# Folding two tiles of squares on VectorE before one ones product, and rounded dummy products in three waits

## The reference, cut to what matters

```python
def rmsnorm(x, g):
    x32 = x.astype(jnp.float32)
    y = x32 * lax.rsqrt(jnp.mean(x32 * x32, axis=-1, keepdims=True) + EPS)
    return (y * g.astype(jnp.float32)).astype(x.dtype)
...
    o = rmsnorm(o_f + o_b, out_g).reshape(B, S, GLA_V)   # 4 heads of 256 values each
    o = o * jax.nn.silu(r.astype(f32))
    return o.astype(h.dtype) @ w_o
```

## Time and profile before

| | |
|---|---|
| runs | 1992.94, 1994.84, 1995.06 us, median 1994.84 |
| profiled execution, span from first to last instruction | 1992.7 us |
| its own time beside the span | none is given apart from the runs; the fastest run is 0.2 us above the span |
| TensorE busy | 1970.7 us, 99% |
| VectorE, ScalarE, GpSimd busy | 57%, 38%, 30% |
| mean granted TensorE clock | 0.998 of full |

### The profile page before, as it was taken

How to read it: one execution, slowest core, us unless ns; L and a number is a source line. 1 busy time by engine, 2 the same in 40 slices (tenths; PEclk the granted TensorE clock), 3 DMA queues, 4 the chain that set the end, 5 groups by cost and what they waited for, 6 DMA issues and landing times.

```text
span 1992.7 us, 24353 instructions
## 1 busy us (share of the span) xinstructions
PE 1970.7 (99%) x9570; PEld 1626.7 (82%) x9570; DVE 1137.4 (57%) x1153; ACT 759.4 (38%) x867; POOL 588.6 (30%) x520
## 2 busy tenths in 40 slices
PE   9999999999999999999999999999999999999998
PEld 7766788888887988888888878788888888888886
DVE  6797355555556547454555466872335474545456
ACT  6665332222234534332322234355553353232223
POOL 1100279997000000289995012522310000000000
PEclk9999999999999999999999999999999999999999
DMA  7300144443223230154443232412123312223231
GB/s 232 101 22 1 63 149 169 153 162 104 102 85 115 86 105 24 66 188 161 143 160 110 96 105 91 117 49 79 64 85 106 106 45 104 102 87 105 84 106 64
DMA packets 32832, 204.01 MB, mean 102 GB/s; under 512 B 3952, under 2 KB 4080, under 8 KB 10096
## 3 DMA queue, kind: packets, MB, share of 16 engines
q1 hardware_dynamic: 25712, 168.83, 24.6%
q0 software_dynamic: 7040, 34.08, 5.4%
HBM read 191.89 MB, written 2.10 MB: 97 GB/s over the span
## 4 chain that ended last, share of the span: by engine, by line
PE 93%; DVE 3%; ACT 2%; issue 1%; DMA 0%; POOL 0%; SPq 0%; POOLq 0%; DVEq 0%; ACTq 0%
PE ps L261 24%; PE ps L263 24%; PE ps L262 24%; PE ps L697 2%; PE ps L2473 2%; PE ps L2474 2%; PE ps L2475 2%; PE ps L1713 1%; PE ps L684 1%; PE ps L293 1%; PE ps L292 1%; PE ps L291 1%; PE ps L1697 1%; PE ps L673 1%; PE ps L672 1%
## 5 line engine op out<-in xcount | busy, mean ns | idle before, releaser
L223 ACT ACTIVATE w_hi<-w_raw 128x2048 fp32r<-128x2048 f32 x142 | 272.4, 1918 | 714.7 <-PE ps L263 643.3
L231 DVE TENSOR_TENSOR w_lo<-w_raw,w_hi 128x2048 fp32r<-128x2048 f32 x139 | 323.2, 2325 | 118.3 <-ACT w_hi L223 116.2
L261 PE MATMUL ps<-h_hi,w_hi 128*128 128x512 f32 (+1 forms) x976 | 383.2, 393 | 4.1 <-DVE w_lo L231 3.0
L263 PE MATMUL ps<-h_hi,w_lo 128*128 128x512 f32 (+1 forms) x976 | 373.5, 383 | 0.0
L262 PE MATMUL ps<-h_lo,w_hi 128*128 128x512 f32 (+1 forms) x976 | 373.3, 383 | 0.0
L1491 POOL TENSOR_SCALAR ada_t<-ada_w,prm 128x256 f32<-128x256 f32 x192 | 219.6, 1144 | 14.0 <-DMA ada_w<-in_ada 13.1
L261 PEld LDWEIGHTS ps<-h_hi,w_hi 128*128 128x128 f32 x976 | 183.6, 188 | 43.9 <-issue 7.7
L263 PEld LDWEIGHTS ps<-h_hi,w_lo 128*128 128x128 f32 x976 | 183.4, 188 | 36.4
L262 PEld LDWEIGHTS ps<-h_lo,w_hi 128*128 128x128 f32 x976 | 183.7, 188 | 34.7 <-issue 1.4
L1019 DVE TENSOR_TENSOR x<-x,ps 128x1024 f32<-128x1024 f32 x128 | 155.8, 1217 | 79.7 <-PE ps L263 79.7
L261 PE MATMUL ps<-m_xhi,w_hi 128*128 128x512 f32 x512 | 200.0, 391 | 0.0
(11 more groups left out here) (348 smaller groups left out, 3205.3 us busy)
## 6 DMA issues: line engine op xcount, KB each, us to landing
w_raw<-in_wb SPq DMA_DIRECT2D x153, 1024.0 KB, 4.9
ada_w<-in_ada POOLq DMA_DIRECT2D x24, 1024.0 KB, 5.3
a_sw<-a_g POOLq DMA_DIRECT2D x20, 128.0 KB, 2.7
x<-in_xT SPq DMA_DIRECT2D x4, 512.0 KB, 7.1
ada_w<-ada_acc POOLq DMA_DIRECT2D x4, 384.0 KB, 5.4
x_rot<-x_g POOLq DMA_DIRECT2D x12, 128.0 KB, 2.7
out<-f_pad SPq DMA_DIRECT2D x3, 512.0 KB, 2.6
w_raw<-in_wb SPq DMA_DIRECT2D x4, 256.0 KB, 6.2
```

The source lines that it names most:

```text
L223: act.activation(w_hi[:, slot], w_raw[:, slot], ACT.Copy).then_inc(hi_done, 1)
L231: dve.tensor_tensor(w_lo[:, slot], w_raw[:, slot], w_hi[:, slot].bitcast(F32), ALU.subtract).then_inc(split_done, 1)
L261: pe.matmul(out, w[0], h[0], start=start, stop=False)
L263: return pe.matmul(out, w[1], h[0], start=False, stop=stop)
```

## The change

1. `sums(h)` waits for a second step of `g_sq` per head and makes one product of `ones` with the first half of `sq`. The second step comes from a new VectorE instruction `folded(h)`, which adds the second half of `sq` to the first (128x512, float32). VectorE has it at the head of turn h + 1, before `states(h + 1, 0)`; for the last head behind the loop, before `root`.
2. The dummy products: behind the second MLP 13 float32 ones become 14 rounded ones with 512 moving columns; ahead of the FFN 12 become 14; at the start 30 become 14 float32 ones followed by 15 rounded ones, which read a tile that VectorE fills first (a new memset of 128x1024, behind a wait for GpSimd's memset of `ones`; TensorE waits for it).

```diff
+        def warm_products(pe, banks, weights, moving, times, rows=slice(0, P)):
+            for t in range(times):
+                w = weights[t % len(weights)]
+                out = ps[0:w.shape[-1], banks[t % len(banks)], 0:S]
+                if len(moving.shape) == 3:
+                    out = out.rearrange("p (a b) -> p a b", a=moving.shape[1])
+                pe.matmul(out, w[rows], moving[rows], start=True, stop=True)
...
-            keep_warm(pe, 7, 13)
+            one, other, moving = ml["m_hi"][:, 0, 0, 0:P], ml["m_lo"][:, 0, 0, 0:P], ml["m_hi"][:, 0, 1, :]
+            warm_products(pe, (7,), (one,), moving, 5)
+            warm_products(pe, (7,), (one[:, 0:64],), moving, 5)
+            warm_products(pe, (7,), (one, other), moving, 4)
...
             def sums(h):
-                pe.wait_ge(g_sq, h + 1)
-                for i in range(2):
-                    last = pe.matmul(ps[:, half_of(h) + 2, :], ones[:], sq[:, 0, i * S:(i + 1) * S], start=i == 0, stop=i == 1)
-                last.then_inc(g_ss, 1)
+                pe.wait_ge(g_sq, 2 * h + 2)
+                pe.matmul(ps[:, half_of(h) + 2, :], ones[:], sq[:, 0, 0:S], start=True, stop=True).then_inc(g_ss, 1)
...
+            def folded(h):
+                dve.wait_ge(g_sq, 2 * h + 1)
+                dve.tensor_tensor(sq[:, 0, 0:S], sq[:, 0, 0:S], sq[:, 0, S:2 * S], ALU.add).then_inc(g_sq, 1)
...
             for h in range(GLA_H):
                 if h >= 1:
                     dve.wait_ge(g_O, h)
+                    folded(h - 1)
                 states(h, 0)
...
                     both_ways(h + 1)
+            folded(GLA_H - 1)
             root(GLA_H - 1)
...
-            keep_warm(pe, 2, 12)
+            one, moving = mx["x_mhi"][:, 0, 0:P], mx["x_mhi"][:, 1, :]
+            warm_products(pe, (2,), (one,), moving, 5, rows=slice(0, 64))
+            warm_products(pe, (2,), (one,), mx["x_mhi"][:, 0:4, 0:P], 5)
+            warm_products(pe, (2,), (one[:, 0:32],), moving, 4)
...
     @block.vector
+        dve.wait_ge(e["ones_set"], 1)
+        dve.memset(e["at_"]["a_q2"][:, 0:2, :].bitcast(F32), 0.5).then_inc(e["ones_set"], 1)
...
     @block.tensor
         pe.wait_ge(e["ones_set"], 1)
-        e["keep_warm"](pe, 5, 30)
+        e["keep_warm"](pe, 5, 14)
+        pe.wait_ge(e["ones_set"], 2)
+        warm = e["at_"]["a_q2"]
+        e["warm_products"](pe, (5, 6), (warm[:, 0, 0:P],), warm[:, 1, :], 6)
+        e["warm_products"](pe, (5,), (warm[:, 0, 0:P],), warm[:, 1, :], 5)
+        e["warm_products"](pe, (5,), (warm[:, 0, 0:96],), warm[:, 1, :], 4)
```

## The result

The changed kernel takes 2008.1 us (median of 5 runs, 2006.27 to 2009.19) against 1994.84 before: ratio 1.007, 95% interval [1.0059, 1.008], slower by 13.3 us. The forecast was 2003.1 with a range up to 2006.8, so the direction and the place were right and the size was not. The profiled execution has a span of 2007.5 us, 14.8 more than before, in a run of 2009.19.

A forecast was written before the change was run, and what follows sets the result against it. It took TensorE's written order as the bound: 1994.84 us plus 8.3 (6.6 net for the heads' stalls, 1.7 for one fall of the clock, 0 for the dummy products) gave 2003.1 us, range 1999.4 to 2006.8.

The forecast's parts named there:

- The stall: GLA heads 0 to 2: TensorE waits 3.26 us for VectorE's add, 2.5 us net a head, 7.5 us together.
- stall, no lapse: Rival: the GLA heads' waits cost +6.6 us net and the clock stays full, 2001.4 us; chance 0.24.
- The last head: Last GLA head: the add is hidden behind 12 projection products, with 0.9 us to spare; a gain of 0.86 us.
- I count one lapse, +1.7 us: GLA heads: the granted clock falls once over the three waits, costing 1.7 us; bounds 0 and 5.1 us.
- two or three lapses: Rival: the clock falls at two or three GLA heads, +3.4 or +5.1 us, 2004.8 or 2006.5 us; chance 0.20.
- the prediction's own bounds: GLA heads: at most 8.1 us and at least 6.5 for the waits; 0 to 5.1 us for the clock.
- The dummy products: Second MLP, FFN and start: new dummy products cost 0 us, kept range 0 to +2, at 0.225 us a product.
- the 0.3 that I gave: Sign: at the three dummy places the first real product starts within 0.3 us of before, shifted by the heads.
- The hidden rival: GLA heads: VectorE reaches the add before TensorE reaches `sums`, gaining 3.4 us, 1991.4 us; chance 0.04, plus 0.03 without the clock's fall near 1190.

The follow-up runs named there:

- the filled kernel: Full change plus 14 float32 dummy products ahead of TensorE's wait for the add at heads 0 to 2: 2001.82 us, ratio 1.0035 to the kernel before.
- between the copies: Full change with VectorE's add of head h - 1 moved between the two copies of within(h): 1992.88 us, ratio 0.9992 to the kernel before.
- the heads alone: Only the edit at the GLA heads, with the old dummy products: 2004.54 us, ratio 1.0053 to the kernel before; timed again 2008.74 us, ratio 1.0066.

## Why the prediction was right or wrong

- **The stall: right.** It named the add as queued behind `both_ways`, a stall of 3.26 us and 2.5 us net a head; measured 3.2, and a turn 2.52 us longer where the clock held. With the stall filled the kernel took 2001.82, where "stall, no lapse" said 2001.4.
- **The last head: right.** There is no wait there, and its product takes 0.86 us. The gain of 0.86 was taken from the sum as said.
- **The clock: the step that failed.** The term "I count one lapse, +1.7 us" was too small in its number and in its price. In the profiled execution there were three lapses in the heads, and each cost more than 1.7: the first 16.84 - 14.18 = 2.66 us, all three about 8.2. The sum fits: 3 x 2.52 for the stalls and 8.2 for the lapses, less 0.86, is 14.9, against a span 14.8 us longer. The price of 1.7 came from the lapse near 1190, whose low stretch was 3.4 us long, all in work. That size exists behind a stall too, and costs 1.5 to 1.65 there. But where the clock fell 0.8 to 1.1 us before the stall's end, the low stretch was 6.8 us, in all seven cases that the traces hold, and cost 2.66 to 2.85 (the last turn against its 11.09 us in the filled kernel). I had one size of lapse in the trace and took it for the price.
- **The number of lapses.** I wrote that the stall is longer than the stretch of near idleness that had cost the clock once, and still counted one in three. By the Trainium skill, "TensorE: Matmul & The Clock Gate", section "HAM oscillation — how this bites in real kernels", it would be every turn. The waits of that section's kernel are some 3 to 5 us, so it is no firm rule for 3.2. Here three of four profiled executions lost the clock at all three heads, and one at one of three, so the measured number varies. The rival "two or three lapses" was the nearer one, at 2006.5 with the old price, and with the measured price 1994.84 + 6.6 + 8.0 = 2009.4. Lapses of varying number and size fit the spread of 6 us in the repeated full change: its five times rise from 2003.13 to 2009.38 us as the mean clock falls from 0.997 to 0.994. Why the clock falls at one place or another of the same stall stays open.
- **The range.** Its lower end took the least stall and the spread of the runs, its upper end neither. With the prediction's own bounds, 8.1 us of stalls and 5.1 of lapses, it would have ended at 1994.84 + 8.1 - 0.9 + 5.1 = 2007.1, and with the same 1.0 of spread at 2008.1.
- **A reading.** The longest wait in front of a product before was 1.7 us (line L638, for `a_sq`), not 1.4. The clock stayed full behind it, so nothing hangs on this.
- **The dummy products: right in sum.** Alone they change nothing (1.0001). Their own time was a little off: 0.25 us each ahead of the FFN where I took 0.225, so the first real product there came 0.55 us late and not within the 0.3 that I gave.
- **The hidden rival was too high in its gain.** It gave 3.4 us; with the add truly hidden between the copies it was about 1.2 to 1.6, not told from nothing by its interval, as VectorE's states bound the turn too. The row for it stood in the trace: 0.16 us of idle time before the first states.
- **The loss of the kernel as it stands** (13.3 us by the medians): 7.6 from the stalls, less 0.9, which leaves some 6.6 for the clock. The kernel with the stall filled agrees: it lost 7.0 (ratio 1.0035), 6.3 less.

## What to carry to other kernels

Moving work from the bound engine to another costs the place in that engine's written order, not the work's length: here an add of 0.68 us, put behind the steps `within`, `queries` and `both_ways`, whose results its reader didn't need, stalled TensorE for 3.2 us. A stall of 2.5 to 4 us on TensorE must be priced with the clock as well, here with nothing, some 1.6 or some 2.8 us more each, and where it can't be removed, dummy products in it take that part away. Before a product is taken out of a loop, look whether another engine ends within some tenths of a microsecond of it: then the gain is little more than that gap.

## What the runs showed of the hardware

- The same stall of 3.2 us cost the clock at three heads of one execution and at one of three in another execution of the same kernel, so its price differs from run to run: 2003.13 to 2009.38 us in five runs, where the kernel before spread over 4 us in 15.
- Low stretches had two lengths. Where the clock fell 0.8 to 1.1 us before the end of a stall they were 6.8 us (seven cases: three in the first profile, three and one in the two of the heads alone). Where it fell as the stall ended or up to 1.2 us behind it they were 3.4 us (the other two in the heads alone, one in the repeated full change, two without dummy products).
- The clock can fall after TensorE has gone back to work: in the heads-alone kernel the ones product at the second head ran at full speed (1.13 us) and the chunk products behind it didn't (4.28).
- Waits of 3.9 and 2.8 us without dummy products each brought a low stretch of some 3.4 us; waits of 2.6 us in the heads brought none in the execution that was profiled, though another run of that kernel had a mean clock of 0.995, and of 0.9 us none.
- GpSimd's add of two 128x512 float32 halves took 1.27 us, VectorE's 0.68.
- 24 products of two columns, 2.7 us back to back, were followed by a low stretch of 3.4 us near 1190 in the kernel before and in most of the profiled executions, but not in three of thirteen (add behind `within`, add on GpSimd in VectorE's old order, no dummy products).
